# The low halves of the up weights: an accumulating DMA in place of a subtraction on VectorE

## The reference

```python
def conv_ffn(x, g, w_up, conv_w, conv_b, w_down, buf):
    t = x.shape[1]
    up = rmsnorm(x, g) @ w_up                        # 1024 -> 2 * 2816
    ext = jnp.concatenate([buf.astype(up.dtype), up], axis=1)
    conv = conv_b + sum(ext[:, i:i + t] * conv_w[i] for i in range(CONV_W))   # width 3
    a, gate = jnp.split(conv, 2, axis=-1)
    y = (jax.nn.silu(gate) * a) @ w_down             # 2816 -> 1024
    return y, ext[:, t:]
```

## Time and profile before

| | us |
|---|---|
| median of 3 runs | 1478.48 |
| lowest and highest run | 1466.24 to 1486.55 |
| the profiled execution, its own time | 1470.2 |
| its span, first to last instruction | 1468.5 |
| its mean granted TensorE clock | 0.965 |

### The profile page before, as it was taken

One profiled execution on the slowest core, in us unless ns is written; L12 is line 12 of the kernel. 1 busy time (PEld: TensorE's weight loads), 2 busy tenths in 40 slices (PEclk: granted clock), 3 DMA queues, 4 the chain that ended last, 5 costly groups with the idle time before them and its releaser, 6 DMA issues.

```text
span 1468.5 us, 24237 instructions
## 1 busy us (share of the span) xinstructions
PE 1402.7 (96%) x8753; PEld 1271.9 (87%) x8753; DVE 942.8 (64%) x1412; ACT 463.4 (32%) x711; POOL 186.3 (13%) x245
## 2 busy tenths in 40 slices
PE   6899999969898999999999999999999999999999
PEld 4678887756665666899999999999999999999999
DVE  6758889876676685744765646556564746465654
ACT  6413121164455555522432222122222212121220
POOL 5540024332221243000000000000000000000000
PEclk9899999987888799999999999999999999999999
DMA  8248766687875776341001202020201102020203
GB/s 280 56 143 262 221 179 186 186 234 214 255 237 184 250 219 178 94 154 29 29 29 58 72 15 72 15 87 1 87 29 58 58 29 72 15 72 15 81 7 127
DMA packets 125536, 168.62 MB, mean 115 GB/s; under 512 B 22789, under 2 KB 99998, under 8 KB 125010
## 3 DMA queue, kind: packets, MB, share of 16 engines
q1 hardware_dynamic: 100988, 129.44, 28.6%
q0 software_dynamic: 7616, 22.03, 5.1%
q10 hardware_dynamic: 16814, 15.62, 3.5%
HBM read 153.09 MB, written 13.96 MB: 114 GB/s over the span
## 4 chain that ended last, share of the span: by engine, by line
PE 77%; DVE 9%; issue 4%; POOL 3%; DMA 2%; SPq 2%; ACT 1%; ACTq 1%; POOLq 0%; DVEq 0%
PE ps L1106 18%; PE ps L1105 18%; PE ps L1107 18%; PE ps L1003 4%; PE ps L1028 2%; PE ps L985 2%; PE ps L903 2%; PE ps L970 2%; PE ps L904 2%; PE ps L905 2%; POOL rsn L2313 1%; PE ps L969 1%; PE ps L1007 1%; PE ps L871 1%; DVE hlo L1625 1%
## 5 line engine op out<-in xcount | busy, mean ns | idle before, releaser
L1105 PE MATMUL ps<-hhi,uhi 128*128 128x344 f32 x1056 | 338.0, 320 | 0.0
L1106 PE MATMUL ps<-hlo,uhi 128*128 128x344 f32 x1056 | 336.5, 319 | 0.0
L1107 PE MATMUL ps<-hhi,ulo 128*128 128x344 f32 x1056 | 336.3, 318 | 0.0
L1105 PEld LDWEIGHTS ps<-hhi,uhi 128*128 128x128 f32 x1056 | 198.2, 188 | 0.5 <-issue 0.5
L1106 PEld LDWEIGHTS ps<-hlo,uhi 128*128 128x128 f32 x1056 | 198.2, 188 | 0.5 <-issue 0.5
L1107 PEld LDWEIGHTS ps<-hhi,ulo 128*128 128x128 f32 x1056 | 198.2, 188 | 0.0
L2222 DVE TENSOR_TENSOR uu<-ps,rstd_bc 128x1032 f32<-128x1032 f32 x44 | 54.2, 1233 | 202.4 <-PE ps L1107 202.2
L903 PE MATMUL ps<-whi,hhi 128*128 128x512 f32 (+1 forms) x376 | 145.9, 388 | 13.5 <-DVE wlo L1619 8.3
L1106 PE MATMUL ps<-alo,dhi 128*128 128x344 f32 x480 | 153.9, 321 | 0.0
L1107 PE MATMUL ps<-ahi,dlo 128*128 128x344 f32 x480 | 153.2, 319 | 0.0
L1105 PE MATMUL ps<-ahi,dhi 128*128 128x344 f32 x480 | 153.1, 319 | 0.0
(11 more groups left out here) (291 smaller groups left out, 2412.9 us busy)
## 6 DMA issues: line engine op xcount, KB each, us to landing
fst<-in_w_upL SPq DMA_DIRECT2D x44, 512.0 KB, 3.5
ring<-in_cache_a_k SPq DMA_DIRECT2D x168, 128.0 KB, 2.6
vring<-in_cache_a_v POOLq DMA_DIRECT2D x128, 128.0 KB, 3.3
vring<-in_cache_a_v SPq DMA_DIRECT2D x104, 128.0 KB, 3.0
ring<-in_cache_a_k ACTq DMA_DIRECT2D x88, 128.0 KB, 2.8
fst<-in_w_down SPq DMA_DIRECT2D x22, 512.0 KB, 3.5
wst<-in_w_in SPq DMA_DIRECT2D x32, 256.0 KB, 3.7
x<-in_xT SPq DMA_DIRECT2D x16, 258.0 KB, 3.7
```

The lines of the kernel that those rows point to most:

```text
L1105: pe.matmul(out, lhs_hi(kc), rhs_hi(kc)[:, cs], start=(n == 0), stop=False)
L1106: pe.matmul(out, lhs_hi(kc), rhs_lo(kc)[:, cs], start=False, stop=False)
L1107: i = pe.matmul(out, lhs_lo(kc), rhs_hi(kc)[:, cs], start=False, stop=(n == nk - 1))
```

## The change

For the 36 up pieces of groups 2 to 10, the low half is made in another way. ScalarE reads the piece a second time and writes minus the rounded value to `ulo`. GpSimd waits for that (`u_neg`) and issues an accumulating DMA, `ulo` plus `fst`, whose completion (`u_lo`) says that the low half is ready and the slot free. It then waits for that completion before it takes the next piece. VectorE's 36 subtractions are left out. SyncE and TensorE wait for `u_lo` where they waited for `f_split`. The 8 up pieces of groups 0 and 1 and all down pieces go the old way. To free two semaphores, `k_mul` and `s_rc` are counted on `dve_chain` now; these waits of VectorE on itself stand where they stood.

SyncE's loads of the pieces:

```diff
             for G in range(1, NGRP - 1):
                 for i in range(6):
-                    sp.wait_ge(S("f_split"), G * 6 + (i + 1))
+                    if i < 2:
+                        if G > 1:
+                            sp.wait_ge(S("u_lo"), 16 * (4 * (G - 2) + 3 + i))
+                        else:
+                            sp.wait_ge(S("f_split"), 7 + i)
+                    elif i < 4:
+                        sp.wait_ge(S("f_split"), 8 + 2 * (G - 1) + i - 1)
+                    else:
+                        sp.wait_ge(S("u_lo"), 16 * (4 * (G - 1) + i - 3))
                     if i < 2:
                         f_piece(i, dnL[G * 2 + (i - 2)])
```

TensorE's units up and down:

```diff
                 for k in range(4):
-                    if k < 2:
-                        pe.wait_ge(S("f_split"), 6 * G + 2 * k)
+                    if k < 2 and G == 1:
+                        pe.wait_ge(S("f_split"), 6 + 2 * k)
+                    elif k < 2:
+                        pe.wait_ge(S("u_lo"), 16 * (4 * (G - 2) + 2 * (k + 1)))
...
-                pe.wait_ge(S("f_split"), 6 * G + 4)
+                pe.wait_ge(S("f_split"), 8 + 2 * G)
                 pe.wait_ge(S("a_split"), 2 * G)
```

ScalarE:

```diff
                         w("f_pe", 7 + i // 2, 12)
                         up_hi(i, fst[:, i % 2])
+                        v = (slice(None), i // 2, slice(4 * (i % 2), 4 * (i % 2) + 4))
+                        act.activation(ulo[v].rearrange("p k c -> p (k c)"), fst[:, i % 2], ACT.Copy, scale=-1.0).then_inc(S("u_neg"), 1)
```

VectorE:

```diff
                         add_down(w, d)
                         if ups and d < KC - 1:
-                            w("f_hi", 10 + d - 2, 6)
-                            up_lo(d - 3, fst[:, (d - 3) % 2])
+                            pass
```

GpSimd, behind its last instruction of before:

```diff
+            for n in range(4 * (NGRP - 2)):
+                v = (slice(None), n % 4 // 2, slice(4 * (n % 2), 4 * (n % 2) + 4))
+                pool.wait_ge(S("u_neg"), n + 1)
+                pool.dma_start(ulo[v].rearrange("p k c -> p (k c)"), fst[:, n % 2], accum_op=ALU.add).then_inc(S("u_lo"), 16)
+                pool.wait_ge(S("u_lo"), 16 * (n + 1))
```

More of the change, by code:

```diff
@@ L725, in _ @@
             for i in range(4):
+                if i < 2:
+                    sp.wait_ge(S("u_lo"), 16 * (4 * (NGRP - 3) + 3 + i))
+                else:
+                    sp.wait_ge(S("f_split"), 8 + 2 * (NGRP - 2) + i - 1)
                 p = 8 + 6 * (NGRP - 2) + i
-                sp.wait_ge(S("f_split"), p - 1)
                 f_piece(p, dnL[2 * (NGRP - 2) + i])
@@ L1194, in _ @@
                     down(d, 1 - G % 2).then_inc(S("f_pe"), 1)
-            pe.wait_ge(S("f_split"), 6 * NGRP)
+            pe.wait_ge(S("f_split"), 8 + 2 * (NGRP - 2) + 4)
             pe.wait_ge(S("a_split"), 2 * NGRP)
@@ L1652, in second_half @@
                 dve.wait_ge(S("rs_row"), 2)
+            multiplied = {}
             def k_mul(n):
                 kv = ring[:, n % 4]
-                dve.tensor_tensor(kv, kv, qb[:, n // 8:n // 8 + 1, :].broadcast_to([P, 4, WG]), ALU.mult).then_inc(S("k_mul"), 1)
+                dve.tensor_tensor(kv, kv, qb[:, n // 8:n // 8 + 1, :].broadcast_to([P, 4, WG]), ALU.mult).then_inc(S("dve_chain"), 1)
+                chain[0] += 1
+                multiplied[n] = chain[0]
             def k_sum(n):
@@ L1825, in granule @@
                     k_mul(n)
-                    dve.wait_ge(S("k_mul"), n + 1)
+                    dve.wait_ge(S("dve_chain"), multiplied[n])
                     k_sum(n)
@@ L1957, in out @@
                 if two(g // NT):
-                    dve.reciprocal(rc[:, g % 2, 0:1], ps[:, 6, HD:HD + 1]).then_inc(S("s_rc"), 1)
-                    T_.wait("s_rc", g + 1)
+                    dve.reciprocal(rc[:, g % 2, 0:1], ps[:, 6, HD:HD + 1]).then_inc(S("dve_chain"), 1)
+                    chain[0] += 1
+                    T_.wait("dve_chain", chain[0])
                     dve.tensor_scalar(oN[:, qtile(g), col:col + HD], ps[:, 6, 0:HD], rc[:, g % 2, 0:1],
@@ L1963, in out @@
                     z = ps[:, 6, 0:2 * (HD + 1)].rearrange("p (a e) -> p a e", a=2)
-                    dve.reciprocal(rc[:, g % 2, :].unsqueeze(2), z[:, :, HD:HD + 1]).then_inc(S("s_rc"), 1)
-                    T_.wait("s_rc", g + 1)
+                    dve.reciprocal(rc[:, g % 2, :].unsqueeze(2), z[:, :, HD:HD + 1]).then_inc(S("dve_chain"), 1)
+                    chain[0] += 1
+                    T_.wait("dve_chain", chain[0])
                     dve.tensor_tensor(oN[:, qtile(g), col:col + 2 * HD].rearrange("p (a e) -> p a e", a=2), z[:, :, 0:HD],
@@ L2073, in _ @@
                     n = K_STEP[g - 1]
-                    T_.wait("k_mul", n + 1)
+                    T_.wait("dve_chain", multiplied[n])
                     k_sum(n)
```

## The result

| | before | changed |
|---|---|---|
| median of 3 runs, us | 1478.48 | 1506.49 |
| lowest and highest | 1466.24 to 1486.55 | 1496.87 to 1519.2 |
| profiled execution, its span | 1470.2, 1468.5 | 1506.49, 1504.9 |
| mean granted clock | 0.965 | 0.957 |

The ratio is 1.0226, with a 95% interval from 1.0159 to 1.0294: slower, clear of no change, though the interval leaves open on which side of 2% it lies. 1512 was stated, 1462 to 1620 the range.

The account below looks back on a forecast made before the run. PE was taken to bound the stage, busy 612.0 of 612 us. Nine groups × (1.9 lateness + 1.8 loads + 0.6 clock) = 39 us on 1470.2 gave 1509, stated as 1512 because its median neighbour lay higher; range 1462 to 1620.

Parts of the forecast that it names:

- "faster" rival: Feed-forward units down: without VectorE's subtractions, PE's matmuls lose memory contention of 1.0 ns each, 1.3 us won; chance 0.02.
- margins and due times: Group boundary: half 0 due at 1035.8, half 1 at 1047.1; VectorE's subtractions were 6.0 and 11.4 us ahead.
- strictly serial chain: GpSimd's four accumulations per boundary, one after the other: end at 1030.6 + 3L for L below 5.6 us, above that 1025.0 + 4L.
- ScalarE's Copies: Feed-forward net: ScalarE's second Copy per piece, 36 × 1.05 us more, costs nothing by itself because ScalarE has room.
- L: Time of one accumulating DMA from GpSimd's issue to GpSimd's release: 6.0 us; waits are zero up to 5.4.
- second pass: Part of the accumulating DMA's time: fetching the destination too, 1.7 us on top of a plain 4.3.
- load term: Second to fourth accumulations each run beside a load of `fst`: 0.6 us each, 1.8 a group.
- "hidden": Rival at group boundaries: the new route fits the margins, L at most 5.4; 1470, up to 1499; chance 0.35.
- lateness of the chain: PE's wait for the low halves at each group boundary: 1.9 us plus 1.8 for the loads.
- clock term: PE's granted clock falling behind the new gaps: 0.6 us a group, with 0 and 5.1 as ends.
- the clock rival: PE's clock falls at each group boundary, up to 5.1 us more, partly covering half 1's wait; 1549 us, chance 0.10.
- "Slow adding": Rival for the accumulating DMAs: read, read and write without overlap, L = 9.4, half 1 15.5 us late; 1626 us, chance 0.17.

Follow-up runs that it names:

- the changed kernel once more: The changed kernel run again with no edit, against the kernel before: median of 6 runs 1499.01 us, ratio 1.0185; nine steps 638.4 us.

## Why the prediction was right

**PE bounds the stage, and VectorE's relief is worth nothing.** Shown: 610.34 us with the subtractions cut to 8 columns. The "faster" rival, 1.3 us from the pace of the units down, is out as well; their 157.7 ns are not VectorE's doing.

**The margins and due times.** They held: half 0 at 12.8 and half 1 at 24.1 us after the first `uhi`. The strictly serial chain held too. Four DMAs in a row make half 1 late, two in flight remove the wait, four more in the row add 21.5 us.

**ScalarE's Copies at nothing.** 0.5 us in nine steps.

**L, and the luck in it.** The forecast 6.0 equals the measured median landing, but L was meant without the loads beside it, and that is 4.8. I put a plain DMA from GpSimd at 4.3; it is 3.15 alone. The 4.7 of the row that I leaned on was a load, in a stage with busy queues; which of the two made it longer is not shown. The second pass, put at 1.7, is 1.3, with 0.3 more for the issue. And the load beside, put at 0.6 us for each of three, costs 1.5 to 1.9 (6.3 and 6.6 against 4.8, two issues of one boundary). So the chain read above took 4.8 + 6.6 + 6.3 + 7.1 = 24.8 us (the last with a packet of instructions in it) where the forecast had 4 × 6.0 + 1.8 = 25.8. L was too long by 1.2 and the load term too short by about as much, and that they made up for each other is luck. With L = 4.8 and 0.6 a load, the prediction's own formula ends at 1030.6 + 3 × 4.8 + 1.8 = 1046.8, before the due time of 1047.1, and would have said "hidden". Only with the load term at its measured size is the chain late.

**The sum.** 39 us was stated, 27.6 and 28.1 measured in the loop: 3.1 a group against 4.3. That 1506.49 came within 6 us of 1512 is in part luck too: between the two profiled executions 8.7 of the 36.4 us lie ahead of the loop, and 1512 itself stands 3 us above the sum of 1509 with no working for it. (A slip beside this: 3 us a group lost would make 1497 for the hidden case, not 1499.) The lateness of the chain was put at 1.9 + 1.8 = 3.7; the waits are 24.6 / 9 = 2.7. Most of the gap is this term, oversized by 1.0. The clock term of 0.6 was near: in the changed kernel two windows of 20 us, of thirty from 830 to 1430, show less than full clock,

```profile
1130.00:1150.00 20.00, 17.18 (x101) 16.89 (x100) 6.51 (x9) 4.21 (x4) 0.86 (x1) 0.91 0.48 133
1330.00:1350.00 20.00, 18.12 (x105) 17.83 (x104) 3.70 (x3) 4.93 (x5) 2.58 (x3) 0.91 0.69 153
```

which is 2 × 0.09 × 20 = 3.6 us, 0.4 a group. The two waits in them (windows of 4 us gave 0.71 and 0.86 around the first, 0.89 and 0.69 around the second):

```profile
1138.09 0.66 PE L1116 MATMUL ps<-hhi,uhi 128*128 128x344 f32 x1 [2.82 <-DMA ulo<-fst]
...
1338.78 0.42 PE L1116 MATMUL ps<-hhi,uhi 128*128 128x344 f32 x1 [1.88 <-DMA ulo<-fst]
```

The 2.10 us at 1066.57, shown above, cost no clock. In the changed kernel once more the clock fell once, behind a wait of 1.97 us, and not behind one of 2.59:

```profile
972.05 0.42 PE L1116 MATMUL ps<-hhi,uhi 128*128 128x344 f32 x1 [1.97 <-DMA ulo<-fst]
...
1186.12 0.43 PE L1116 MATMUL ps<-hhi,uhi 128*128 128x344 f32 x1 [2.59 <-DMA ulo<-fst]
```

```profile
970.00:990.00 20.00, 18.03 (x105) 17.84 (x105) 6.21 (x9) 6.98 (x7) 1.72 (x2) 0.91 0.62 160
1180.00:1200.00 20.00, 16.43 (x103) 15.86 (x102) 5.15 (x7) 5.39 (x6) 2.16 (x3) 1.00 0.70 161
```

All three drops follow an accumulation of 7.65 to 7.80 us with a packet of instructions in it. The wait at 1338.78 stood before k = 0, and before k = 1 of that boundary there was none: it is the one that is missing from 18. The slower k = 0 had covered it, as the clock rival had it. Together, 24.6 us of waiting and 3.6 of clock make 28.2, near the 27.6 of the loop. In the repetition it is 26.2 and 1.8, 28.0 beside 28.1.

**The rivals.** "Hidden" fell because the accumulations beside a load took 6.3 us or more at the boundary read; L alone, 4.8, is under the 5.4 and even under the 5 that it needed. By the estimate of 4.4 us from the Trainium skill ("DMA: Bandwidth & Descriptors", anatomy of one DMA on the GpSimd path, with "Collectives: The Full Stack", the bandwidth ceiling) it would have held. A DMA that runs alone came near it, 4.8 us; the three that run beside a load did not, and there are four in a row. That a second source is read and the add itself is nearly free, as the Trainium skill says in the second page, agrees with the 1.3 us more behind the issue and with twice the busy time of the DMA engines (2.8 against 1.4 us). "Slow adding" at 9.4 is out. "Clock falling at each boundary" is out too: it fell at two of nine, and at one of nine in the repetition.

## What to carry to other kernels

The bound engine never waited here, so moving work from a second engine to a third had nothing to win and could only lose. Before such a move, read how early the old way delivered (here 6.0 and 11.4 us) and add up the new chain against that, with the price of each DMA beside the transfers that it will meet, not the price of one alone. A DMA that its issuer waits for before the next counts with its whole latency, and again with every transfer that it lets loose; with one semaphore for each slot and two in flight, the same work disappeared from the time. Even then it gained nothing over the kernel before, because there was nothing to gain.

## What I had not expected of the hardware

An accumulating DMA of 512 KB from SBUF to SBUF takes 4.8 us from issue to next issue when alone, a plain one 3.15; GpSimd's issue itself is 0.86 us for one and 0.53 for the other. A load of 512 KB beside it adds 1.3 to 2.0 us to the accumulation. Where one packet of 16 KB of instructions fell into an accumulation that ran alone, it took 0.6 to 1.9 us more; the waits behind which the clock fell in the changed kernel had such a packet before them. PE's clock fell after waits of 2.82, 1.88 and 1.97 us inside unbroken matmuls and stayed after 2.10 and 2.59, so the length of a wait of 2 to 3 us does not settle it. And executions of these kernels differ by up to 19 us in one place that the change does not touch: the attention stage, in step with the clock that PE is granted there (0.81 to 0.89). Measuring steps inside the loop made 0.5 us visible where whole times scatter by 26 (1462.54 to 1488.74 in 17 runs).
